# Moving the second view of TensorE's activation buffer: 256 bytes behind the first in place of 320

## The reference, cut to what matters

```python
def _swiglu(t, w_gate, w_up, w_down):
    return (jax.nn.silu(t @ w_gate) * (t @ w_up)) @ w_down
...
        f = _swiglu(_rmsnorm(h, ffn1_pre_g[l]), ffn1_w_gate[l], ffn1_w_up[l], ffn1_w_down[l])
        h = h + 0.5 * _rmsnorm(f, ffn1_post_g[l])
        u = _rmsnorm(h, mix_pre_g[l])
        proj = u @ w_in[l]
...
def conv_ffn(x_n, w_up, conv_w, w_down):
    g, u = jnp.split(causal_dwconv(x_n @ w_up, conv_w), 2, axis=-1)
    return (jax.nn.silu(g) * u) @ w_down
```

## Time and profile before

| what | value |
|---|---|
| median of three runs | 1843.75 us (1843.71 to 1844.1) |
| profiled execution, first to last instruction | 1842.3 us |
| mean granted TensorE clock | 0.999 |
| matmul records, weight-load records | 10951, 10951 |
| VectorE, ScalarE, GpSimd busy | 70%, 59%, 11% |
| DMA, read from memory | 330.97 MB, mean 181 GB/s |

### The profile page before, as it was taken

The page is one execution under the profiler, slowest core; times in us unless marked ns, Lnnn a source line. Parts: engine busy times, 40 slices in busy tenths (PEclk is TensorE's granted clock), DMA queues, the critical chain, the costliest instruction groups (busy, mean ns, idle before and its releaser), DMA issues.

```text
span 1842.3 us, 28823 instructions
## 1 busy us (share of the span) xinstructions
PE 1829.0 (99%) x10951; PEld 1633.5 (89%) x10951; DVE 1287.1 (70%) x2041; ACT 1090.7 (59%) x1885; POOL 205.1 (11%) x158
## 2 busy tenths in 40 slices
PE   8999999999999999999999999999999999999998
PEld 7888999998888888888999888888889998989997
DVE  6775747787777568755777788755768765768763
ACT  7665545555666466645555657655557654757653
POOL 0220001110022002200011102210002210001210
PEclk9999999999999999999999999999999999999999
DMA  9755565455576558664654548654747654537663
GB/s 268 216 186 183 172 194 171 140 158 176 173 225 192 189 148 233 186 193 139 196 176 143 186 146 230 193 190 144 226 139 215 187 195 155 173 115 205 198 192 103
DMA packets 435721, 333.94 MB, mean 181 GB/s; under 512 B 25338, under 2 KB 381312, under 8 KB 435584
## 3 DMA queue, kind: packets, MB, share of 16 engines
q1 hardware_dynamic: 435008, 331.57, 59.7%
q10 hardware_dynamic: 576, 0.53, 0.1%
HBM read 330.97 MB, written 1.05 MB: 180 GB/s over the span
## 4 chain that ended last, share of the span: by engine, by line
PE 96%; DVE 2%; ACT 1%; issue 0%; DMA 0%; ACTq 0%
PE bank L1759 16%; PE bank L1736 15%; PE bank L1738 15%; PE bank L1737 15%; PE bank L1747 7%; PE bank L1761 7%; PE bank L1748 7%; PE bank L1749 7%; PE bank L1765 2%; PE bank L1758 1%; DVE wlo L1106 1%; PE bank L2017 0%; DVE U L1159 0%; PE bank L2083 0%; PE bank L2088 0%; PE bank L2054 0%
## 5 line engine op out<-in xcount | busy, mean ns | idle before, releaser
L1106 DVE TENSOR_TENSOR wlo<-raw,whi 128x1024 fp32r<-128x1024 f32 (+3 forms) x637 | 760.9, 1202 | 286.3 <-ACT whi L578 276.8
L578 ACT ACTIVATE whi<-raw 128x1024 fp32r<-128x1024 f32 (+3 forms) x637 | 645.6, 1023 | 324.6 <-PE bank L1738 247.9
L1759 PE MATMUL bank<-U,whi 128*128 128x512 f32 x1280 | 439.2, 395 | 0.2 <-DVE wlo L1106 0.2
L1761 PE MATMUL bank<-U,wlo 128*128 128x256 f32 x1120 | 314.6, 281 | 0.0
L1747 PE MATMUL bank<-U,whi 128*128 128x256 f32 x1024 | 289.2, 282 | 0.0
L1748 PE MATMUL bank<-U,whi 128*128 128x256 f32 x1024 | 286.1, 279 | 0.0
L1749 PE MATMUL bank<-U,wlo 128*128 128x256 f32 x1024 | 286.0, 279 | 0.0
L1759 PEld LDWEIGHTS bank<-U,whi 128*128 128x128 f32 x1280 | 230.2, 188 | 42.9 <-DVE wlo L1106 0.7
L1736 PE MATMUL bank<-whi,U 128*128 128x384 f32 (+2 forms) x592 | 219.2, 370 | 2.7 <-DVE wlo L1464 2.1
L1736 PE MATMUL bank<-whi,hhi 128*128 128x512 f32 x560 | 219.3, 392 | 0.0
L1738 PE MATMUL bank<-wlo,hhi 128*128 128x512 f32 x560 | 218.1, 390 | 0.0
(11 more groups left out here) (309 smaller groups left out, 2367.4 us busy)
## 6 DMA issues: line engine op xcount, KB each, us to landing
raw<-in_ffn_w_up SPq DMA_DIRECT2D x351, 256.0 KB, 3.5
raw<-in_ffn_w_down SPq DMA_DIRECT2D x264, 256.0 KB, 2.9
raw<-in_ffn_w_gate SPq DMA_DIRECT2D x175, 256.0 KB, 3.4
raw<-in_w_gate SPq DMA_DIRECT2D x128, 192.0 KB, 2.9
raw<-in_w_in SPq DMA_DIRECT2D x80, 256.0 KB, 3.4
raw<-in_a_w_in SPq DMA_DIRECT2D x48, 256.0 KB, 3.2
raw<-in_w_mem_kv SPq DMA_DIRECT2D x32, 256.0 KB, 3.3
raw<-in_w_out SPq DMA_DIRECT2D x32, 256.0 KB, 3.1
```

What stands on the lines that cost most here:

```text
L578: act.activation(whi[n % SLOTS][:, 0:w], raw[n % RAW][:, 0:w], ACT.Copy).then_inc(hi_ready, 1)
L1106: dve.tensor_tensor(wlo[n % SLOTS][:, 0:w], raw[n % RAW][:, 0:w], whi[n % SLOTS][:, 0:w].bitcast(F32), ALU.subtract).then_inc(lo_ready, 1)
L1759: ins = pe.matmul(dst, wh, u2[:, k, :], start=(k == 0), stop=(k == KT - 1))
L1761: pe.matmul(dst[:, 0:TOK], wl, uhi[:, k, :], start=False, stop=False)
```

## The change

The further view of `U` begins 64 columns (256 bytes) behind the nearer one, and no longer 80 columns (320 bytes). The buffer keeps its size, so no other buffer moves. The instructions of all five engines and their order stay the same (PE 10226 rows, VectorE 1435, ScalarE 1207, with none changed); only the addresses of the U operands in all blocks but 6 and 8 are other ones.

```diff
         U = sb("U", [P, 2 * KT * TOK + 80], F32R)
         ucols = lambda at: U[:, at:at + 2 * KT * TOK].rearrange("p (k n) -> p k n", k=KT)
-        u0, u2 = ucols(0), ucols(80)
+        u0, u2 = ucols(0), ucols(64)
         uhi, ulo = u2[:, :, 0:TOK], u2[:, :, TOK:2 * TOK]
```

## The result

The changed kernel is slower: its median is 1852.44 us (1851.21 to 1852.71, four runs) against 1843.92 us of the kernel before, run beside it. The ratio is 1.0042, with a 95% interval of 1.003 to 1.0054. The forecast was +3.8 us and 1847.5 us, its range ended at 1851.5 us. The sign of what was forecast is right, the size is about half of what came, and the time lies outside the range.

The account below looks back on a forecast made before the run. PE, running its matmuls one behind the other, was taken to bound the kernel; 7.1 - 2.5 - 0.6 - 0.2 + 0 = +3.8 us, so 1843.75 to 1847.5 us, with an 8 in 10 range of 1841.5 to 1851.5.

Parts of the forecast that it names:

- Step 1: Projections of 256 columns in the further view slow to 119.9 ns, from 117.8 or 113.3: +7.1 us.
- Rival B: The distance does not matter and both views run alike: 0 us, 1843.75 us; chance 0.08.
- rival D: At 256 bytes projections keep 117.8 ns while stationary uses and wide pairs settle: -8.2 us, 1835.6 us; chance 0.05.
- step 4: Wide projections, 1280 pairs of one 512 and one 256 columns, stay near 350 ns a pair: 0 us.
- A: Rival: wide pairs settle at distance 0, 346.6 ns, -4.9 us more, 1842.6 us in all; chance 0.25.
- C: Rival: wide pairs alternate worse at distance 0, 355 ns: +5.9 us, in all +9.7, 1853.5 us; chance 0.12.
- Step 2: 480 matmuls with U stationary and 512 columns get faster by 5.4 ns each: -2.5 us.
- Step 3: U stationary in the gates, 768 matmuls of 384 columns: -0.6 us; 288 matmuls of 344 columns: -0.2 us.

Follow-up runs that it names:

- e3: The changed kernel with 64 bytes of unused space ahead of every buffer, so addresses move and distances do not; ratio 1.0039 to the kernel before.
- e1: The kernel before with the further view of U at 256 bytes in blocks 7 and 9 only; ratio 1.0021, +3.9 us.
- e2: The kernel before with the further view of U at 256 bytes in blocks 0 and 3 only; ratio 1.0004.
- e5: The kernel before (320 bytes) with the wide projections grouped, eight matmuls of 512 columns, then eight of 256; ratio 0.9961, -7.2 us.
- e6: The changed kernel (256 bytes) with wide projections grouped, eight of 512 columns, then eight of 256; ratio 1.0017 to the kernel before, +3.1 us.
- e11: The kernel before with wide projections grouped by width, blocks 7 and 9 at 32 bytes and block 6 at 192; ratio 0.995, -9.2 us.

## Why the prediction was wrong

**What held.** That PE's pace sets the time, that it depends on the distance of its operands modulo 256 bytes, and that the signs differ by use. e3 shows the distance, e1 and e2 show that the parts add up block by block. Step 1, the projections: +7.1 us forecast, +7.2 measured, with 117.8 to 120.0 ns and 113.3 to 119.8 in the stretches named. A little of that agreement is luck, because how many stretches of the mixers run at 113.3 ns changes from one execution to the next: of the eight with 46 matmuls that the earlier trace rows is one of, five did in the trace of before and four in that of e1 and of e2, with equal code and addresses there. The Trainium skill, "SBUF — State Buffer", section "SBUF: two separate sides", has TensorE never waiting on anyone at its ports. Taken to mean that the place of an operand is free, the rule does not agree with these stretches: an alternating pair of the same two matmuls took between 347.5 and 353.3 ns by distance alone, all at the full granted clock, while VectorE's and ScalarE's busy times in the two kernels compared stayed the same to 0.2 us. Whether any port is waited for is a question that the runs leave open. What the two operands do to one another, in the memory or in the engine, no run here shows either; the runs move addresses and order, and see the time alone. Rival B (no effect) and rival D (projections keep their pace) are excluded by the same rows.

**What failed: step 4, the wide pairs**, "I expect an alternation to stay unsettled at either distance, near 350 ns, and take 0". It stays unsettled, but not near 350: 352.5 ns, +2.1 a pair, +2.5 to 2.7 us. The lower case, A, that the pairs settle at 346.6, did not come either. The premise of step 4 was that an unsettled pair costs the same at either distance; e2 shows in one execution that it does not, 352.5 ns in block 3 and 350.4 in block 2. C came nearest, a pair over 351 ns, with a chance of 0.12. In the trace after, over the 303 pairs of block 2, the distance from the start of a matmul of 512 columns to the next start is 235.1 ns (231.6 before), which is the 235 ns of C's bound; but from a start of 256 columns it is 117.4 ns (118.8 before) and not the 120 that C put beside it, so that the cost is less than half of C's. One such pair in the trace after:

```profile
520.51 0.40 PE L1759 MATMUL bank<-U,whi 128*128 128x512 f32 x1
520.75 0.28 PE L1761 MATMUL bank<-U,wlo 128*128 128x256 f32 x1
520.86 0.40 PE L1759 MATMUL bank<-U,whi 128*128 128x512 f32 x1
```

The rows held a better estimate than 0: the five matmuls behind a change of width gave 232.0 and so 352 a pair, and I set that aside for the belief that both distances are alike when unsettled. That 352 comes so close is luck in part, since its two terms, 232.0 and 120, are not the two measured. Nor does the alternation explain why 256 bytes are slower than 320: e5 and e6 are without it, and there the nearer distance costs 4.6 ns a pair, 349.2 against 344.6, more than twice the 2.1 ns.

**Smaller misses.** Step 2, U stationary with 512 columns: -2.5 forecast (480 x 5.4 ns is 2.6), -2.0 measured outside block 0. The pace itself fell as forecast, to 227.8 ns; the blocks of 24 with a wait at their head keep less of it. Step 3, the gates: -0.6 forecast, -0.3 measured; 344 columns -0.2 and -0.3. Steps 2 and 3 together left out some 0.7 us of gain. No wait grew, as forecast.

**The sum.** 3.8 forecast; +2.5 (step 4), +0.5 (step 2), +0.3 (gates) and the tenths of the projections and of 344 columns make +7.1 us, against 7.7 by the ratio (5.5 to 10) and 8.5 between the medians. The profiled execution has another 1.2 us at its start, where its clock fell for 3.4 us. The range was too narrow on this side because it went only "the larger part of the way to C", though the upper bound of a single term, 5.9 us, was its own reason to go all the way.

## What to carry to other kernels

Where TensorE is the bound and its matmuls run back to back, the place of an operand in its partition relative to the other operand is worth up to 7 ns a matmul, and it can be read from the trace as the distance of starts in dense stretches, by use and shape. A term for which no row exists (here alternating widths at distance 0) needs its whole bound in the range, and a run that measures that order itself, because neither the distance nor the order of the matmuls can be judged without the other. Put matmuls of one width together and measure: here that gave 7 us at 320 bytes, about as much as the change cost, but at 32 bytes it made the pairs slower.

## What the runs showed of the hardware

Two things I had not expected. At one distance a stretch of equal matmuls can run at more than one settled pace: 113.3 and 117.8 ns at 320 bytes, 113.4 and 117.8 at 192, 116.7 and 117.8 at 32. Which of them a stretch has is not set by code and addresses alone: the third long projection stretch of block 1, 46 matmuls at 320 bytes, has 113.3 ns in the traces of before and e5 and 117.8 ns in those of e1, e2 and e11. And the paces themselves are exact from run to run: the wide pairs of block 2 took 106.18 us in three traces at 320 bytes (before, e1, e2), and 106.81 us in two at 256 (after, e3), to the hundredth of a microsecond, so that a difference of 0.1 ns a matmul is visible in a trace where the intervals of the timed runs are 2 us wide or more. Why a stretch enters one pace or the other stays open; no run here isolates it.
